# First stage of a two-block layer kernel: gate weights loaded second, squares folded by VectorE, gate and angle arithmetic spread over later panels

## What is computed

```python
h = x * rsqrt(mean(x*x, channels) + eps) * norm_mix_w      # x: 256 tokens, 2048 channels
y = h @ w_in                                               # q, k, v, z, 2 x 16 gate columns, ...
qkv = silu(conv1d_5taps(y[q, k, v]))                       # per channel, along the tokens
z   = silu(y[z])
g    = -exp(a_log) * softplus(y[gate columns 0:16] + dt_bias)
beta = sigmoid(y[gate columns 16:32])
cos, sin = cos(positions * freq), sin(positions * freq)    # for the attention that comes later
```

## Time and profile before

| what | value |
|---|---|
| runs | 3722.78, 3725.10, 3725.49 us, median 3725.10 |
| the profiled execution's own time | 3721.84 us |
| its span in the profile | 3720.0 us |
| TensorE busy | 3516.5 us, 95% of the span |
| VectorE busy | 2236.7 us, 60% |
| ScalarE busy | 1548.3 us, 42% |
| GpSimd busy | 251.9 us, 7% |
| mean granted TensorE clock | 0.98 of full speed |

### The profile page before, as it was taken

One profiled execution on the slowest core, in us unless ns is written; L12 is line 12 of the kernel. 1 busy time (PEld: TensorE's weight loads), 2 busy tenths in 40 slices (PEclk: granted clock), 3 DMA queues, 4 the chain that ended last, 5 costly groups with the idle time before them and its releaser, 6 DMA issues.

```text
span 3720.0 us, 80273 instructions
## 1 busy us (share of the span) xinstructions
PE 3516.5 (95%) x35914; PEld 3176.6 (85%) x35914; DVE 2236.7 (60%) x3384; ACT 1548.3 (42%) x2397; POOL 251.9 (7%) x302
## 2 busy tenths in 40 slices
PE   7999989999989999999999999999999999999988
PEld 7898988888878888888888888988888888888877
DVE  6655756655655788885545445355565656556555
ACT  4333333333324444444434444333554444444333
POOL 0011002100000000000001010001201101101000
PEclk9999999999999999999999999999999999999989
DMA  4533543375434555555454333434433333333254
GB/s 169 190 144 121 183 180 123 146 286 199 167 122 159 179 189 191 193 187 198 170 179 151 110 134 132 148 127 164 151 110 108 125 111 104 122 103 113 102 209 147
DMA packets 94391, 571.46 MB, mean 154 GB/s; under 512 B 12689, under 2 KB 20913, under 8 KB 32097
## 3 DMA queue, kind: packets, MB, share of 16 engines
q1 hardware_dynamic: 80496, 511.85, 39.2%
q0 software_dynamic: 13552, 54.49, 4.4%
HBM read 536.01 MB, written 30.28 MB: 152 GB/s over the span
## 4 chain that ended last, share of the span: by engine, by line
PE 82%; DVE 9%; ACT 5%; DMA 2%; issue 2%; POOL 0%; SPq 0%; DVEq 0%; ACTq 0%; POOLq 0%
PE banks L284 16%; PE banks L285 8%; PE banks L2039 4%; PE banks L273 3%; PE banks L274 3%; PE banks L275 3%; PE banks L306 3%; PE banks L307 3%; PE banks L308 3%; PE banks L979 3%; PE banks L2040 3%; PE banks L2041 3%; PE banks L980 3%; PE banks L981 3%; PE banks L2236 2%
## 5 line engine op out<-in xcount | busy, mean ns | idle before, releaser
L253 DVE TENSOR_TENSOR w_lo<-ring,w_hi 128x2048 fp32r<-128x2048 f32 x274 | 629.5, 2297 | 449.5 <-ACT w_hi L247 449.2
L247 ACT CAST w_hi<-ring 128x2048 fp32r<-128x2048 f32 x274 | 522.9, 1908 | 237.6 <-PE banks L285 112.4
L284 PE MATMUL banks<-x_two,w_hi 128*128 128x512 f32 x1408 | 489.6, 394 | 0.3 <-PE banks L1065 0.3
L285 PE MATMUL banks<-x_two,w_lo 128*128 128x256 f32 x1408 | 390.6, 277 | 0.0
L2095 DVE TENSOR_TENSOR w_lo<-ring,w_hi 128x512 fp32r<-128x512 f32 x316 | 217.1, 688 | 246.8 <-ACT w_hi L2052 245.8
L979 PE MATMUL banks<-x_two,w_hi 128*128 128x256 f32 x1152 | 349.5, 303 | 7.2 <-DVE w_lo L1046 7.2
L980 PE MATMUL banks<-x_two,w_hi 128*128 128x256 f32 x1152 | 331.8, 288 | 0.0
L981 PE MATMUL banks<-x_two,w_lo 128*128 128x256 f32 x1152 | 331.4, 288 | 0.0
L2039 PE MATMUL banks<-XK,w_hi 128*128 128x256 f32 x1024 | 316.8, 309 | 11.4 <-DVE w_lo L2095 11.4
L284 PEld LDWEIGHTS banks<-x_two,w_hi 128*128 128x128 f32 x1408 | 264.7, 188 | 62.3 <-issue 0.7
L2040 PE MATMUL banks<-XK,w_hi 128*128 128x256 f32 x1024 | 290.0, 283 | 2.7 <-issue 2.7
(11 more groups left out here) (535 smaller groups left out, 8323.9 us busy)
## 6 DMA issues: line engine op xcount, KB each, us to landing
ring<-in_w_up SPq DMA_DIRECT2D x88, 1024.0 KB, 4.9
ring<-in_w_dil SPq DMA_DIRECT2D x72, 1024.0 KB, 5.0
mod_ring<-in_w_mod SPq DMA_DIRECT2D x48, 1024.0 KB, 7.4
ring<-in_w_logit SPq DMA_DIRECT2D x48, 1024.0 KB, 4.9
ring<-in_w_down SPq DMA_DIRECT2D x44, 1024.0 KB, 4.9
ring<-in_w_delta SPq DMA_DIRECT2D x32, 1024.0 KB, 4.9
ring<-in_w_out SPq DMA_DIRECT2D x32, 1024.0 KB, 4.9
ring<-in_w_na SPq DMA_DIRECT2D x32, 1024.0 KB, 4.8
```

What stands on the lines that cost most here:

```text
L247: nc.scalar.copy(w_hi[:, s, 0:w], ring[:, s, 0:w]).then_inc(S("panel_hi"), 4)
L253: nc.vector.tensor_tensor(w_lo[:, s, 0:w], ring[:, s, 0:w], w_hi[:, s, 0:w].bitcast(F32), ALU.subtract).then_inc(S("panel_split"), 1)
L284: nc.tensor.matmul(out_ap, hi, both, start=first_, stop=False)
L285: return nc.tensor.matmul(out_ap[:, 0, :], lo, both[:, 0, :], start=False, stop=last_)
```

## The change

Ten edits, all in the first stage:

1. SyncE's order becomes small, x part 0, gate panel, x parts 1 to 3, delta panels. GpSimd issues its two small loads first, waits until the gate panel has landed, and then issues the constants. TensorE waits for the constants after the gate panel and no longer before it.
2. ScalarE does a one-column Copy as soon as `small` is there, splits panel 0 after x part 0, and does the split of panel 2 ahead of the squares.
3. VectorE clears `CC` at the start, splits panel 0 after x part 0.
4. TensorE waits for x_lo tile by tile in the gate panel.
5. VectorE copies the gate panel out unscaled, and adds the four square results to one tile of 256 columns (three additions of 1024 columns, one of 512, one of 256). TensorE sums that one tile with ones in the middle of panel 2 (step k = 1), after its ninth tile.
6. The root of the mean is worked out in step k = 0 of the delta stage, on both engines, after the split of panel 3; panel 1's result is copied out unscaled and scaled afterwards.
7. The gate rows are transposed by TensorE right behind panel 2 (step 1), once VectorE has scaled them in step 0. In steps 0 to 4 of `delta0` VectorE splits panel p + 2 first and convolves afterwards; step 0's convolution is done in step 1, after the transposes.
8. Gate arithmetic: VectorE four pieces in step 3 and two in step 10, ScalarE two Exp in step 4, Ln in step 6, Sigmoid in step 8.
9. Angles: two of VectorE's 16 operations in each step from 4 on; ScalarE's Silu of the condition in step 2, its two Sin in step 15.
10. ScalarE's Silu of step k comes after the split of step k + 1 instead of waiting in step k (both delta stages).

```diff
     def start_act(act):
         act.wait_ge(S("small_loaded"), 16)
+        nc.scalar.activation(scratch, small[:, 0:1], ACT.Copy)
         for j in range(4):
...
-            if j == 1:
+            if j == 0:
                 act_split(act, (0, None, 0))
-            if j == 3:
-                act_split(act, (1, None, 0))
+        act_split(act, (1, None, 0))
+        tick(act, act_split, (0, None, 0))
         for j in range(4):
             nc.scalar.activation(sq[:, 4 * j:4 * j + 4, :], x[:, 4 * j:4 * j + 4, :], ACT.Square).then_inc(S("sq_ready"), 1)
-        root_act(act, 1, RS[0][:, :])
...
         nc.vector.tensor_copy(GF1, g_fin)
-        root_dve(dve, ch, 1, RS[0][:, :])
+        p = (first["gates"], None, 0)
+        dve.wait_ge(S("panel_used"), at(p, 3))
+        ch(nc.vector.tensor_copy(qkv[:, 0, :], pbank(p)))
+        dve.sem_inc(S("proj_read"), 1)
+        tick(dve, dve_split, p)
+        for j in range(1, 4):
+            dve.wait_ge(S("sq_ready"), j + 1)
+            ch(nc.vector.tensor_tensor(sq[:, 0:4, :], sq[:, 0:4, :], sq[:, 4 * j:4 * j + 4, :], ALU.add))
+        ch(nc.vector.tensor_tensor(sq[:, 0:2, :], sq[:, 0:2, :], sq[:, 2:4, :], ALU.add))
+        nc.vector.tensor_tensor(sq[:, 0, :], sq[:, 0, :], sq[:, 1, :], ALU.add).then_inc(S("sq_folded"), 1)
...
-        for k in range(KT):
-            if k % 4 == 0:
-                pe.wait_ge(S("sq_ready"), k // 4 + 1)
-            last = nc.tensor.matmul(banks[0][:, 0:T], C("ones"), sq[:, k, :], start=k == 0, stop=k == KT - 1)
-        last.then_inc(S("ss_ready"), 1)
+
+    def start_sum(pe):
+        pe.wait_ge(S("sq_folded"), 1)
+        nc.tensor.matmul(banks[0][:, 0:T], C("ones"), sq[:, 0, :], start=True, stop=True).then_inc(S("ss_ready"), 1)
+
+    def gates_turn(pe):
         pe.wait_ge(S("gate_step"), 1)
         for t in range(TT):
             last = nc.tensor.transpose(banks[0][:, t * P:(t + 1) * P], qkv[:, 0, t * P:(t + 1) * P], C("ident"))
...
     def delta_pe(pe, it, fill):
-            project(pe, p, rhs_x, pbank(p))
+            project(pe, p, rhs_x, pbank(p), middle=start_sum if it == 0 and k == 1 else None)
+            if it == 0 and k == 1:
+                gates_turn(pe)
...
     def delta_act(act, it, fill):
+        for k in range(16):
+            p = (first[f"delta{it}"] + k, None, 0)
+            tick(act, act_split, p)
+            if it == 0 and k == 0:
+                root_act(act, 1, RS[0][:, :])
+            if k:
+                gate(k - 1)
+            if it == 0:
+                gates_act(act, k)
+                angles_act(act, k)
+        gate(15)
...
     def delta_dve(dve, ch, it, fill):
+            if it == 0 and k == 0:
+                nc.vector.tensor_copy(dst, pbank(p)).then_inc(S("proj_read"), 1)
+                tick(dve, dve_split, p)
+                root_dve(dve, ch, 1, RS[0][:, :])
+                nc.vector.tensor_tensor(qkv[:, 0, :], qkv[:, 0, :], RS[0][:, :], ALU.mult).then_inc(S("gate_step"), 1)
+                dve.wait_ge(S("proj_read"), at(p, 3))
+                ch(nc.vector.tensor_tensor(dst, dst, RS[0][:, :], ALU.mult))
+                continue
             nc.vector.tensor_tensor(dst, pbank(p), RS[0][:, :], ALU.mult).then_inc(S("proj_read"), 1)
...
+            if it == 0 and k <= 4:
+                tick(dve, dve_split, p)
+                if k == 1:
+                    dve.wait_ge(S("gate_step"), 2)
+                    convolve(0)
+                convolve(k)
+            else:
+                if k < 12:
+                    convolve(k)
+                tick(dve, dve_split, p)
+            if it == 0:
+                gates_dve(dve, ch, k)
+                for _ in range(2 if k >= 4 else 0):
+                    next(angles, None)
```

More of the change, by code:

```diff
@@ L261, in tick, with project @@
         split(eng, ahead(p), w)
-    def project(pe, p, rhs, out_ap, tiles=KT, ready=None):
+    def project(pe, p, rhs, out_ap, tiles=KT, ready=None, middle=None):
         s = p[0] % 2
@@ L275, in project @@
             last = nc.tensor.matmul(out_ap, lo, xh, start=False, stop=k == tiles - 1)
+            if middle and k == tiles // 2:
+                middle(pe)
         last.then_inc(S("panel_used"), 1)
@@ L546, in gates_dve, with gates_act @@
[L546 to L555, removed]
-        ga = gates_f[:, :, 0:16]
[L557 to L564, removed]
+    def gates_act(act, k):
+        if k == 4:
+            act.wait_ge(S("gate_step"), 3)
+            nc.scalar.activation(gtmp[:, :, 0:16], gtmp[:, :, 0:16], ACT.Exp).then_inc(S("gate_step"), 1)
+            nc.scalar.activation(alog, alog, ACT.Exp).then_inc(S("gate_step"), 1)
+        if k == 6:
+            act.wait_ge(S("gate_step"), 5)
+            nc.scalar.activation(gtmp[:, :, 0:16], gtmp[:, :, 0:16], ACT.Ln, bias=1.0).then_inc(S("gate_step"), 1)
+        if k == 8:
+            nc.scalar.activation(beta[:, :, 0:16], banks[0][:, 0:TT * P].rearrange("p (t c) -> p t c", t=TT)[:, :, 16:32],
+                                 ACT.Sigmoid).then_inc(S("gate_step"), 1)
@@ L668, in delta_act, with gate @@
         F = filler(fill)
-        for k in range(16):
-            p = (first[f"delta{it}"] + k, None, 0)
-            tick(act, act_split, p)
+        def gate(k):
             if k < 12:
@@ L675, in delta_act @@
             else:
-                act.wait_ge(S("proj_read"), at(p, 3))
+                act.wait_ge(S("proj_read"), at((first[f"delta{it}"] + k, None, 0), 3))
                 nc.scalar.activation(zg[:, k - 12, :], zg[:, k - 12, :], ACT.Silu).then_inc(S("z_gate"), 1)
+        for k in range(16):
[9 more added lines that the diff above has]
+        gate(15)
         n1 = lambda k, per: at((k, it, per))
@@ L734, in delta_dve, with convolve @@
         F = filler(fill)
+        angles = angles_dve(dve, ch)
+        def convolve(k):
+            dve.wait_ge(S("proj_read"), at((first[f"delta{it}"] + k, None, 0), 3))
+            w = lambda j: cw_qkv[:, it * 60 + k * 5 + j:it * 60 + k * 5 + j + 1]
+            ch(nc.vector.tensor_scalar(qkv[:, k, :], raw[:, k, 0:T], w(0), None, ALU.mult))
+            for j in range(1, 5):
+                last = nc.vector.scalar_tensor_tensor(qkv[:, k, :], raw[:, k, j:j + T], w(j), qkv[:, k, :],
+                                                      ALU.mult, ALU.add)
+                if j < 4:
+                    ch(last)
+            last.then_inc(S("convolved"), 1)
         dve.wait_ge(S("delta_done"), 1 + at((0, it, 1)))
@@ L741, in delta_dve @@
             dst = raw[:, k, 2:2 + T] if k < 12 else zg[:, k - 12, :]
-            nc.vector.tensor_tensor(dst, pbank(p), RS[0][:, :], ALU.mult).then_inc(S("proj_read"), 1)
[L743 to L753, removed]
+            if it == 0 and k == 0:
[6 more added lines that the diff above has]
+                continue
+            nc.vector.tensor_tensor(dst, pbank(p), RS[0][:, :], ALU.mult).then_inc(S("proj_read"), 1)
+            if it == 0 and k <= 4:
+                tick(dve, dve_split, p)
+                if k == 1:
+                    dve.wait_ge(S("gate_step"), 2)
+                    convolve(0)
[8 more added lines that the diff above has]
+                    next(angles, None)
         n1 = lambda k, per: at((k, it, per))
@@ new lines, in angles_act @@
+    def angles_act(act, k):
+        if k == 2:
+            act.wait_ge(S("side_loaded"), 32)
+            act.wait_ge(S("cond_clear"), 1)
+            nc.scalar.activation(CC[:, :, 0:2], cond_in[:, :].rearrange("p (k c) -> p k c", c=2), ACT.Silu).then_inc(S("cond_ready"), 1)
+        if k == 15:
+            act.wait_ge(S("angles"), 1)
+            nc.scalar.activation(cos0[:, :], cos0[:, :], ACT.Sin).then_inc(S("angles"), 1)
+            nc.scalar.activation(sin0[:, :], sin0[:, :], ACT.Sin).then_inc(S("angles"), 1)
@@ L2973, in _ @@
                 load((0, None, 0), a["w_gates"][0, :, :])
-                load_x(sp, 2)
-                load_x(sp, 3)
+                for j in range(1, 4):
+                    load_x(sp, j)
             elif name in ("delta0", "delta1"):
@@ L3093, in _ @@
         pool.dma_start(pos_i[:, :], a["pos"]).then_inc(S("side_loaded"), 16)
+        pool.wait_ge(S("panel_loaded0"), 16)
+        load_first(pool)
         for it in range(2):
```

62 lines of the change are left out of this document (32 added, 30 removed).

## The result

The changed kernel took 3705.93 us (median of 4 runs, 3702.70 to 3710.74), the kernel before beside it 3725.3 (3722.78 to 3735.97). The medians lie 19.4 us apart. The ratio of the two sets is 0.9937, 95% interval 0.9919 to 0.9955: 23 us less, between 17 and 30. Its profiled execution took 3710.74 us, span 3708.9, only 11.1 us less than the one of before. So one gain has several sizes; most of this study is about why.

What follows compares the result with a forecast made beforehand. TensorE was taken to set the pace, with 38.5 us before panel 16's end being start, waits, squares and low clock. 18.6 + 0.4 - 1.7 = 17.3 us gained; 3725.1 - 17.3 = 3708 us, range 3702 to 3715.

Steps and rivals of the forecast that it cites:

- E: End of panel 16 on TensorE, in the first stage; forecast at about 119 us against 136.36 before.
- the three signs named: On TensorE: about 2 us waiting ahead of the transposes, panel 3 at 35 us, about 1 us waiting near 66.
- Gate panel lands at 8.0: Start of the first stage: gate panel's load landing at 8.0 us instead of 11.54, bounds 7 and 11.5.
- first matmul: TensorE's start on the gate panel, after cast and subtraction of panel 0: 12.2 us instead of 15.9.
- panel 3's start: TensorE starting panel 3 after the transposes: 35.2 us instead of 53.84, a gain of 18.6 us.
- Clock, 1.5 us charged to panel 3: TensorE's clock falling after the new 2 us wait: 1.5 us lost against 1.9 before, 0.4 better.
- the rule weighed in the prediction: Slower case: frequent short TensorE waits make its clock fall repeatedly; 3744 us with eight slow panels, chance 0.03.
- VectorE's lateness, 1.7 us: VectorE's added load in the delta steps: 1.1 + 0.2 + 0.4 us lost, bounds 0.5 and 4.
- The rival of the clock staying high: TensorE's clock not falling after the 2 us wait: 1.5 us more gained, 3706.5 us, chance 0.10.
- The one of the load order: Rival: the gate panel doesn't land earlier than 11.54 us; gain 15 us, 3710 us, chance 0.12.
- the term for what lies behind E: Everything after panel 16: assumed only to move along with its end, adding no gain or loss.
- The later stretches: Later low-clock stretches behind the first stage's panels falling otherwise: plus or minus 3 us.

Runs made afterwards that it cites:

- the changed kernel's fifth profile: The changed kernel, unedited, profiled once more; own time 3713.27 us, panel 16 ending at 120.91 us.

## Why the prediction was right and wrong

- *That it is faster, and by which mechanism*: right. E came 17.4 us earlier, with 17.3 worked out, and the three signs named (panel 3 near 35: 36.5; a wait of 2 us before it: 2.67; a wait near 66 us of 1 us: 0.93 at 66.49) were there, as was VectorE without idle time in steps 5 to 11.
- *Gate panel lands at 8.0*: 9.1. I took the bytes that had moved by a time and let 0.36 MB of overlap stand. By 9.1 us 289 GB/s x 9.1 us = 2.63 MB had moved, where small, x part 0, the gate panel and the two small inputs are 1.86 MB, so 0.77 MB of later loads had come early. The step "first matmul" was 1.2 us short, and panel 3's start came at 36.5, not 35.2: of the 18.6 us 17.3 came.
- *Clock, 1.5 us charged to panel 3*: in the first profile none was lost, 1.9 gained against before instead of 0.4. This error and the last one cancelled, and that E agrees within 0.1 us is luck. In the changed kernel's fifth profile the 1.5 us were lost as charged, and E is 120.91. By the rule weighed in the prediction, the Trainium skill's TensorE: Matmul & The Clock Gate, "A second HAM failure mode", frequent short idles would have made the clock go back and forth; the first profile doesn't agree: with the one wait of 0.93 us the clock stayed at 1.00 throughout 36 to 100 us. No run here shows what many such waits would do.
- *VectorE's lateness, 1.7 us*: 0.93 at panel 8, and 52.5 - 51.8 = 0.7 behind it: 1.6. The terms as measured give 17.3 + 1.9 - 1.6 = 17.6; the last 0.2 us went between panels 3 and 8.
- *The rival of the clock staying high* was the true one for its term in four of the changed kernel's five profiles. The one of the load order was priced at 2.3 us and came to about 3.
- *Where it failed*: the term for what lies behind E, and with it the range. The sum put that term at nothing ("if the rest only moves with it"), and the range gave it 3 to 4 us. The first comparison's ratio makes 0.9937 x 3725.3 = 3701.8 us, just under the lower end of 3702, though the medians of those runs and of all 17 (3705.93 and 3704.4) lie inside. "The later stretches" measured more than that: executions of either kernel differ by up to 20 us, through two paces of one stage (9.4 us apart) and through the low-clock stretches of the late stage (918.6 to 927.4 us), where the changed kernel came out 4 us better in the means. Why it did so stays open. I had three runs within 2.7 us before me and took their closeness for the kernel's spread; 63 runs of it reach from 3719.3 to 3739.5.

## What to carry to other kernels

When one engine's waits are removed, work out the next one's load per step before counting the gain: here VectorE had 0.66 us of slack in 5.76 and was given 0.71, and removing TensorE's last visible wait (2.7 us) then returned only a few tenths. Arithmetic on few columns and table changes belong beside panels in pieces (10.2 us here), and best where the receiving engine waits anyway. Read a gain from a fixed point behind the change in several profiles (here it lay within 1.4 us before and 2.0 after), and the whole time only from many runs.

## What the runs showed of the hardware

- TensorE at full granted clock ran one stage of 88 panels in 489.2 to 489.4 us in five of nine profiles and in 498.5 to 498.7 in the other four, of both kernels, with nothing between: 146 or 144 (143) records in 25 us, all of the stage long. The nine profiles of the other versions keep to the same two paces, two at 489 and seven at 498.5 to 498.8. What decides it was not found.
- What a wait of TensorE does to its clock differs between executions of one program. Waits of 2.4 to 2.7 us ahead of the transposes were followed by the upper level in six profiles and by the lower in two (0.68 and 0.66 over the next 4 us). One of 2.0 us was followed by the lower once and once not. Those of 3.3 us and 8.5 us were followed by the lower (0.61 and 0.50 over the next 4 us).
- The constants, issued at about 9 us beside the last x parts, took 9.0 us to land, against 7.3 ahead of them. Panel 1's weights landed at 17.1 us, and at 17.6 with the old order of loads; the forecast had 16.5.
